# Thirty-two single-column products placed between the large products of a projection job

## What is computed

```python
def retention_recurrent(q, k, v, S0):
    g = jnp.exp(log_gammas())[None, :, None, None]
    def step(S, qkv):
        q_t, k_t, v_t = qkv
        S = g * S + jnp.einsum('bhd,bhe->bhde', k_t, v_t)
        return S, jnp.einsum('bhd,bhde->bhe', q_t, S)
...
def layer(h, ...):
    q, k, v, g, a, b = jnp.split(rms_norm(h) @ w_in, ...)
    o, new_ret = retention(...)                  # prompt: chunks of 128; samples: the step above
    ret_out = normed(o) * silu(g)
    mix = concatenate([ret_out, conv_out]) @ w_out
    h = h + rms_norm(mix)
    ... # feed-forward part
```

## Time and profile before

| | |
|---|---|
| median of 3 runs | 1212.38 us (1209.39 to 1212.67) |
| the profiled execution | 1212.49 us, of which its span is 1210.7 us |
| mean granted TensorE clock | 0.991 of full |
| busy share of the span: TensorE, VectorE, ScalarE, GpSimd | 97%, 61%, 34%, 35% |
| instructions of TensorE's matmul side | 8411 |

### The profile page before, as it was taken

The page is one execution under the profiler, slowest core; times in us unless marked ns, Lnnn a source line. Parts: engine busy times, 40 slices in busy tenths (PEclk is TensorE's granted clock), DMA queues, the critical chain, the costliest instruction groups (busy, mean ns, idle before and its releaser), DMA issues.

```text
span 1210.7 us, 21798 instructions
## 1 busy us (share of the span) xinstructions
PE 1179.2 (97%) x8411; PEld 1157.4 (96%) x8411; DVE 741.2 (61%) x1203; ACT 409.4 (34%) x718; POOL 422.9 (35%) x304
## 2 busy tenths in 40 slices
PE   7999999999999998799999999999999999999997
PEld 6999999999999986699999999999999999999997
DVE  5559899944455247965555555655656565656556
ACT  5444444333344245531313131313131313222223
POOL 3066788213122267431313132322222222222226
PEclk9999999999979999899999999999999999999999
DMA  9211111121144233121212020202011121212134
GB/s 311 87 35 53 35 53 53 36 72 36 36 139 114 88 122 116 44 71 36 71 35 69 17 87 0 88 16 86 18 59 45 40 64 35 69 35 69 36 143 173
DMA packets 99797, 84.49 MB, mean 70 GB/s; under 512 B 2722, under 2 KB 89378, under 8 KB 99738
## 3 DMA queue, kind: packets, MB, share of 16 engines
q1 hardware_dynamic: 99554, 83.61, 22.4%
q10 hardware_dynamic: 192, 0.17, 0.0%
HBM read 72.86 MB, written 11.38 MB: 70 GB/s over the span
## 4 chain that ended last, share of the span: by engine, by line
PE 91%; POOL 3%; DVE 3%; issue 2%; DMA 1%; ACT 1%; DVEq 0%; ACTq 0%; POOLq 0%
PE ps L356 28%; PE ps L358 28%; PE ps L357 28%; PE ps L1756 1%; POOL o_last L690 1%; POOL h_ring L663 1%; PE ps L1582 1%; PE ps L1621 1%; PE ps L1686 1%; PE ps L1705 1%; PE ps L1810 1%; PE ps L1809 1%; DMA t_sm<-table_identity_decays 1%; POOL st L546 1%; DVE w_ring L1409 1%
## 5 line engine op out<-in xcount | busy, mean ns | idle before, releaser
L356 PE MATMUL ps<-xn_hi,w_hi 128*128 128x350 f32 (+2 forms) x576 | 187.2, 325 | 0.3 <-DVE xn_lo L1114 0.2
L358 PE MATMUL ps<-xn_lo,w_hi 128*128 128x350 f32 (+2 forms) x576 | 185.2, 322 | 0.0
L357 PE MATMUL ps<-xn_hi,w_lo 128*128 128x350 f32 (+2 forms) x576 | 184.9, 321 | 0.0
L356 PE MATMUL ps<-x_hi,w_ring 128*128 128x256 f32 x616 | 174.2, 283 | 7.2 <-DVE w_ring L1409 6.3
L356 PE MATMUL ps<-x,w_ring 128*128 128x260 f32 x616 | 175.4, 285 | 1.6 <-issue 1.2
L357 PE MATMUL ps<-x,w_ring 128*128 128x260 f32 x616 | 175.3, 285 | 0.0
L358 PE MATMUL ps<-x,w_ring 128*128 128x260 f32 x616 | 175.0, 284 | 0.0
L358 PE MATMUL ps<-x_lo,w_ring 128*128 128x256 f32 x616 | 173.6, 282 | 0.0
L357 PE MATMUL ps<-x_hi,w_ring 128*128 128x256 f32 x616 | 173.5, 282 | 0.0
L356 PE MATMUL ps<-act_hi,fx_hi 128*128 128x388 f32 (+1 forms) x528 | 171.3, 324 | 0.3
L358 PE MATMUL ps<-act_lo,fx_hi 128*128 128x388 f32 (+1 forms) x528 | 168.5, 319 | 0.0
(11 more groups left out here) (232 smaller groups left out, 2496.4 us busy)
## 6 DMA issues: line engine op xcount, KB each, us to landing
f_raw<-in_w_ffn_in SPq DMA_DIRECT2D x42, 512.0 KB, 4.2
raw<-in_w_in SPq DMA_DIRECT2D x24, 512.0 KB, 3.9
f_raw<-in_w_ffn_out SPq DMA_DIRECT2D x22, 512.0 KB, 3.3
x_st<-in_x_prompt SPq DMA_DIRECT2D x8, 512.0 KB, 7.9
raw<-in_w_out SPq DMA_DIRECT2D x8, 512.0 KB, 5.6
h_ring<-in_x_prompt SPq DMA_DIRECT2D x8, 512.0 KB, 4.6
h_scratch<-h_ring SPq DMA_DIRECT2D x8, 512.0 KB, 3.0
h_fin<-h_scratch SPq DMA_DIRECT2D x8, 512.0 KB
```

Source lines behind the costliest of these rows:

```text
L356: nc.tensor.matmul(out, hi, mhi, start=first, stop=False, skip_group_check=resumes)
L357: nc.tensor.matmul(out, lo, mhi, start=False, stop=False, skip_group_check=resumes)
L358: return nc.tensor.matmul(out, hi, mlo, start=False, stop=last, skip_group_check=resumes)
```

## The change

The products of the samples leave chunk 5. `g_job(11)`, in chunk 4, now takes them: behind each of its 24 large matmuls stands a product of the samples, and behind each third one two. The job so waits for all eight state updates and for the normed output of chunk 3. All four counts of `s_os` come with the last product. The state updates are spread in another way. Before, chunk n (1 to 4) made update 2n - 2 ahead of the norm's sums and update 2n - 1 at its end. Now update 0 stands ahead of the sums of chunk 1, updates 2n - 1 and 2n together at the end of chunks 1 to 3, and update 7 ahead of the sums of chunk 4.

```diff
--- before.py
+++ after.py
@@ -1294,8 +1294,10 @@
                     w_split_lo(N_IN + 1)
                 if n == 7:
                     w_split_lo(N_IN + 3)
-                if 1 <= n < 5:
-                    state_update(2 * n - 2)
+                if n == 1:
+                    state_update(0)
+                if n == 4:
+                    state_update(NS - 1)
                 dve.wait_ge(s_sq, n + 1)
                 v.tensor_reduce(st[:, 24:28], sqj[:, :, :], AX_X, ALU.add).then_inc(s_red, 1)
                 dve.wait_ge(s_red, n + 1)
@@ -1318,8 +1320,9 @@
                 ln_shift(n)
                 if n >= 1:
                     ret_out(n - 1)
-                if 1 <= n < 5:
+                if 1 <= n < 4:
                     state_update(2 * n - 1)
+                    state_update(2 * n)
                 if n == 5:
                     ret_lo(0)
                 if n == 6:
@@ -1655,7 +1658,12 @@
             project(4, 5, (s_t1, 24), s_vg, IN_CHUNKS, xn_hi, xn_lo, s_job)
 
 
-            def g_job(j):
+            def sample_o(hh, b):
+
+                return mm(ps[:, 5, hh * NS + b:hh * NS + b + 1], state_sb[:, hh, b, :],
+                          qT[:, hh, META + SEQ + b:META + SEQ + b + 1], start=True, stop=True)
+
+            def g_job(j, samples=False):
 
                 r, (c0, n) = j % H, QG_CHUNKS[j // H]
                 if j == 0:
@@ -1664,9 +1672,24 @@
                     pe.wait_ge(s_wlo, SLOTS + N_IN - SLOTS + r + 1)
                 if j >= 1:
                     pe.wait_ge(s_vg, CREDIT_AB + 12 + j)
+                if samples:
+                    pe.wait_ge(s_vbd, NS)
+                    pe.wait_ge(s_on, 4)
                 for k in range(KT):
-                    ins = three_pass(ps[:, 6, 0:n], w_hi[:, r, k * P:(k + 1) * P], w_lo[:, r, k * P:(k + 1) * P],
-                                     xn_hi[:, k, c0:c0 + n], xn_lo[:, k, c0:c0 + n], k == 0, k == KT - 1)
+                    wh, wl = w_hi[:, r, k * P:(k + 1) * P], w_lo[:, r, k * P:(k + 1) * P]
+                    xh, xl = xn_hi[:, k, c0:c0 + n], xn_lo[:, k, c0:c0 + n]
+                    if not samples:
+                        ins = three_pass(ps[:, 6, 0:n], wh, wl, xh, xl, k == 0, k == KT - 1)
+                        continue
+                    nc.tensor.matmul(ps[:, 6, 0:n], wh, xh, start=k == 0, stop=False, skip_group_check=True)
+                    sample_o(0, k)
+                    nc.tensor.matmul(ps[:, 6, 0:n], wl, xh, start=False, stop=False, skip_group_check=True)
+                    sample_o(1, k)
+                    ins = nc.tensor.matmul(ps[:, 6, 0:n], wh, xl, start=False, stop=k == KT - 1, skip_group_check=True)
+                    sample_o(2, k)
+                    last = sample_o(3, k)
+                if samples:
+                    last.then_inc(s_os, H)
                 ins.then_inc(s_job, 1)
 
             g_job(0)
@@ -1746,16 +1769,6 @@
                 for ct in range(CT):
                     ins = tr(ps[:, 7, ct * P:ct * P + m], yn[0:m, n % 2, ct * P:(ct + 1) * P], ident[0:m, 0:m])
                 ins.then_inc(s_ynT, 1)
-
-            def sample_o(hh):
-
-                if hh == 0:
-                    pe.wait_ge(s_vbd, NS)
-                    pe.wait_ge(s_on, 4)
-                for b in range(NS):
-                    ins = mm(ps[:, 5, hh * NS + b:hh * NS + b + 1], state_sb[:, hh, b, :],
-                             qT[:, hh, META + SEQ + b:META + SEQ + b + 1], start=True, stop=True)
-                ins.then_inc(s_os, 1)
 
             def out_job(i):
 
@@ -1811,17 +1824,11 @@
                 ins.then_inc(s_O, 1)
                 pe.wait_ge(s_ktok, n + 1)
                 kv(kT[:, :, c], vT[:, :, c], P)
-                if n == 5:
-                    sample_o(0)
-                    sample_o(1)
                 if n >= 6:
                     out_job(2 * n - 12)
                 y_tok(n)
-                if n == 5:
-                    sample_o(2)
-                    sample_o(3)
                 if n < 5:
-                    g_job(2 * n + 3)
+                    g_job(2 * n + 3, n == 4)
                 if n >= 1:
                     o_back(n - 1)
                 if n >= 6:
```

## The result

The changed kernel took 1224.3 us (median of 4 runs, 1222.62 to 1224.9). Before took 1211.18 us in the same comparison (4 runs). The ratio is 1.0108 (95% interval 1.0094 to 1.0122): slower by about 13 us, outside the forecast range of 1208 to 1215.5 us.

What follows compares the result with a forecast made beforehand. TensorE's own list was taken to bound the kernel, with 6.4 us lost to the lower clock in chunk 5. Getting that back, less 5.5 us in two waits, gave 0.9 us faster: 1211.6 us, range 1208 to 1215.5.

Steps and rivals of the forecast that it cites:

- The products' own work, 7.1 us in the new place: In g_job(11), 64 passes each cost a weight load of 0.111 us, so the job grows from 3.9 to 11.0 us.
- the hidden loads: Rival: weight loads in the job lie wholly behind the large matmuls, 7.1 us less, 1204.5 us; chance 6%.
- the dear switches: Upper bound in the job: changing between split and plain fp32 data costs a load each time, 2.7 us more.
- The clock inside the job: In g_job(11) the granted clock stays at 1.00, as a large matmul is always in flight or just behind.
- the tail's row: Trace row at the kernel's end, 1202 to 1207 us: 2.34 us of TensorE work in 5 us, clock 1.00.
- the clock falls inside the job: Rival: the job loses the clock as the stretch at 343 us did, +6 us in all, 1218.5 us; chance 10%.
- the first rival: The clock falls in the wait ahead of out_job(0), which then runs slower: +0.6 us, 1213.1 us; chance 28%.
- State updates, SyncE's queue: The moved updates cost 0, with update 7 done 2.5 us ahead of need; output weights are issued as the job ends.
- The first wait, 1.9 us: In chunk 5, TensorE's transposes of k wait 1.9 us for ret_out(4), which the products had covered.
- The second wait, 3.6 us: Ahead of out_job(0), TensorE waits 3.6 us for the weights' split, held up by ret_hi(0) and ret_lo(0).
- The clock in the second wait: The clock falls in the wait ahead of out_job(0), 3.1 us at half rate costing 1.5 us; chance 28%.
- The sum: Of 6.4 us given back by the clock, 5.5 go into the two waits: 0.9 us faster, 1211.6 us.

Runs made afterwards that it cites:

- The fastest variant: The kernel before with products streaming 128 columns at their old place in chunk 5 and earlier splits ahead of the first output job: 1206.49 us, ratio 0.9964.
- e1: The kernel before with only the new distribution of the state updates, products left in chunk 5: 1210.33 us, ratio 0.9997.
- e9: The kernel before with only the earlier splits ahead of the first output job, single-column products at the old place: 1209.9 us, ratio 0.9992.
- e4: The changed kernel, single-column products in the job, with conv_hi(0), ret_hi(0) and conv_lo(0) moved earlier: 1217.07 us, ratio 1.0052.
- e7: The changed kernel with one more wait, so that GpSimd's conv_lo(0) begins after VectorE's ret_lo(0): one execution, 1222.77 us.
- e3: The changed kernel with each product in the job streaming 128 columns, only the last wanted: 1216.15 us, ratio 1.0046.
- e8: The changed kernel with the 32 single-column products in one block directly behind the last gate job in chunk 4: 1220.55 us, ratio 1.008.
- e10: The changed kernel with products of 16 columns in the job: 1216.34 us, ratio 1.0051 (three executions).
- e11: The changed kernel with products of 32 columns in the job: 1216.32 us, ratio 1.0051 (two executions).
- e2: The kernel before with products streaming 128 columns, only the last wanted, at their old place in chunk 5: 1210.67 us, ratio 1.0003.
- e6: The changed kernel with 128-column products in the job and the earlier splits ahead of the first output job: 1210.48 us, ratio 0.9993.

## Why the prediction was wrong

**What bounds the kernel.** Right: TensorE's list alone, and 6.4 us lost to the lower clock. The fastest variant got back 4.3 us in the median (1210.75 to 1206.49) and 6.0 between the profiled executions (1212.49 to 1206.49).

**The products' own work, 7.1 us in the new place.** Right. The job at full clock takes 10.95 us (128, 32 and 16 columns). That rules out the hidden loads and the dear switches alike, and it fits the reasoning that a second load of a pair has nothing to hide behind.

**The clock inside the job: "I take full clock, by the tail's row".** This is the step that failed. The clock fell 6.5 us into the job and stayed low for 13.65 us, worth 6.5 us. The rival "the clock falls inside the job" had it, at 10% and +7 us. I held the job against the kernel's tail and read the tail wrong. Its 2.34 us of work in 5 us are not thin work: they are dense products of 128 columns up to 1204.35 us, and then nothing. And the clock did fall there, 4.7 us after the last of them, just behind the window that I had put in the earlier trace rows. From the same trace of before (TensorE's busy time comes first, the clock behind the five engines):

```profile
1202.00:1204.35 2.35, 2.34 (x21) 2.15 (x20) 2.35 (x3) 0.81 (x2) 1.35 (x3) 1.00 0.55 223
1204.35:1209.05 4.70, 0.00 (x0) 0.00 (x0) 2.99 (x4) 0.00 (x0) 1.91 (x1) 1.00 0.80 312
1209.05:1210.70 1.65, 0.00 (x0) 0.00 (x0) 0.00 (x0) 0.00 (x0) 0.00 (x0) 0.51 0.33 84
```

So the tail spoke neither for a mixed stretch nor against the idle wait of the first rival. The nearest row was the one with the same products, at 343 us, and it spoke against me. With 16 columns in place of one, in the same order and with the same passes, the clock holds. So what was streamed between the loads made the difference, not the mixing.

**State updates, SyncE's queue.** Right. The updates cost nothing (e1), and update 7 began at 329.40 for 330.3. The queue shows in the changed kernel's trace alone: the weights are issued from 348.4 us on, as the job ends, and ScalarE splits them from 363.7 on without waiting for them.

**The first wait, 1.9 us.** Right: 2.06.

**The second wait, 3.6 us.** Mechanism and place right, size wrong: 5.3 us. The term mis-sized is `ret_lo(0)`, taken at 1.75 us from a row in which GpSimd had finished before it began. In the new order the two meet and it takes 3.49. By my own times `conv_hi(0)` ended near 348.7, so GpSimd's 3.2 us of `conv_lo(0)` had to run into the 350.2 at which I let `ret_lo(0)` begin. I did not look at what it does to its neighbour.

**The clock in the second wait.** I gave it 28% and 1.5 us. It fell there, in the changed kernel and wherever that wait stood, and cost 2.6 us, because two thirds of the output job (5.2 of 6.8 us) ran at 0.50.

**The sum.** 0.9 us faster was the difference of a gain of 6.4 and waits of 5.5. The gain did not come at all (the fall inside the job cost 6.5 where before lost 6.4), the waits were 7.0, the second fall added 2.6: 9.7 us slower in the profiled execution. The rivals were priced one at a time. Two of them came together, and the longer second wait with them; the range had no room for that.

One part of the difference is chance. Before's executions spread from 1208.9 to 1213.3 us, with many near 1209.7 and near 1212.4. Two profiled executions near 1212.5 (before and e9) had 13.65 us at the lower clock in this stage, one at 1211.0 (e1) had 10.2. So the 6.4 us that I took for the loss were those of a slower execution; at the same price for each low microsecond, 10.2 us are an estimated 4.8. With single-column products in the job the low stretch was 13.65 us in one profile and 17.1 in two others (e4, e7). Why it is the one or the other in an execution was not tried.

## What to carry to other kernels

A product that streams one column keeps TensorE busy in the profile, but it costs its weight load and can cost the clock. Widening it with columns that nobody reads was free here up to 128 columns and held the clock; mixing it with large products did not hold it. A row that ends in the middle of an idle stretch says nothing of what the clock does next. Before moving work away from where it stands, follow the in-order lists of the other engines: what it covered there is the price, and a duration taken from a row holds only while the same neighbours are at work.

## What the runs showed of the hardware

- A pass of fp32 weights at full clock took 0.111 to 0.112 us with 1 and with 128 columns (2.4 us for 22 passes and 3.58 us for 32), so its streaming was free.
- In the same job, 64 passes of 1 column lost the clock after 6.5 us (changed kernel) and after about 4 (e4, e7), and 64 passes of 16 columns kept it for all of its 10.95 us. TensorE was busy throughout in both.
- The waits of 5.3 to 5.6 us ended at a granted clock of 0.50 in each profile that had one (the changed kernel, e3, e7, e8, e10, e11). A wait of 2.84 us was followed 0.5 us later by 3.4 us at 0.50 (e2), and one of 2.24 by the same 1.4 us later (e6). The first waits of 2.06 and 2.07 us were followed by none before the next wait (the changed kernel, e3, e4, e8).
- With nothing to do after 1204.35 us, TensorE lost the clock 4.7 us later (before).
- VectorE's subtraction on two SBUF operands took 1.75 us alone and 3.49 us when it began under a GpSimd instruction of the same kind. Its neighbours that read PSUM took no longer.
